# Cross attention in three products of high and low parts, with its last steps in another order

## What is computed

```python
q = (h @ w_xq).reshape(B, S, XATT_HEADS, XATT_HEAD_DIM)        # 4 heads of 256
k, v = jnp.split(mem_n @ w_xkv, 2, axis=-1)                    # same heads
s = jnp.einsum('bshd,bmhd->bhsm', q, k) * (XATT_HEAD_DIM ** -0.5)
p = jax.nn.softmax(s, axis=-1)
o = jnp.einsum('bhsm,bmhd->bshd', p, v)
return o.reshape(B, S, D_MODEL) @ w_xo
```

## Time and profile before

| | us |
|---|---|
| runs | 1096.91, 1097.23, 1099.27; median 1097.23 |
| the profiled execution | 1098.35 |
| its span, first to last instruction | 1096.5 |
| TensorE busy in it | 1085.8 (99%) |
| VectorE, ScalarE, GpSimd busy | 613.4, 562.3, 673.1 |
| granted clock of TensorE | 0.999 of full speed |

### The profile page before, as it was taken

One profiled execution on the slowest core, in us unless ns is written; L12 is line 12 of the kernel. 1 busy time (PEld: TensorE's weight loads), 2 busy tenths in 40 slices (PEclk: granted clock), 3 DMA queues, 4 the chain that ended last, 5 costly groups with the idle time before them and its releaser, 6 DMA issues.

```text
span 1096.5 us, 18883 instructions
## 1 busy us (share of the span) xinstructions
PE 1085.8 (99%) x7591; PEld 984.7 (90%) x7594; DVE 613.4 (56%) x1116; ACT 562.3 (51%) x888; POOL 673.1 (61%) x351
## 2 busy tenths in 40 slices
PE   8999999999999999999999999999999999999997
PEld 7999999998898988888899999999988979888886
DVE  6788579355514642346558877783644345323454
ACT  7545854434645544444464567544346554444443
POOL 4876758627674457754477758685277544686442
PEclk9999999999999999999999999999999999999999
DMA  7544545625653655566555545456266355566563
GB/s 291 174 152 137 177 142 163 174 81 158 195 161 122 211 186 183 190 192 187 178 174 173 157 137 170 145 163 155 77 192 193 96 173 182 186 190 191 183 185 113
DMA packets 63333, 183.31 MB, mean 167 GB/s; under 512 B 18576, under 2 KB 19088, under 8 KB 63248
## 3 DMA queue, kind: packets, MB, share of 16 engines
q1 hardware_dynamic: 47936, 172.48, 49.8%
q10 hardware_dynamic: 15312, 9.64, 3.3%
HBM read 179.47 MB, written 2.62 MB: 166 GB/s over the span
## 4 chain that ended last, share of the span: by engine, by line
PE 96%; DMA 1%; DVE 1%; ACT 1%; POOL 0%; issue 0%; SPq 0%; DVEq 0%; ACTq 0%; POOLq 0%
PE psum L521 22%; PE psum L522 21%; PE psum L523 21%; PE psum L550 12%; PE psum L551 6%; PE psum L695 1%; PE psum L1022 1%; PE psum L1001 1%; PE psum L736 1%; DMA sb_raw<-weights 1%; PE psum L1123 1%; PE psum L625 1%; PE psum L916 1%; PE psum L909 1%; PE psum L791 1%; PE psum L719 1%
## 5 line engine op out<-in xcount | busy, mean ns | idle before, releaser
L418 POOL TENSOR_TENSOR sb_low<-sb_raw,sb_high 128x1024 fp32r<-128x1024 f32 x257 | 619.0, 2423 | 331.4 <-ACT sb_high L408 317.3
L408 ACT ACTIVATE sb_high<-sb_raw 128x1024 fp32r<-128x1024 f32 x322 | 340.2, 1061 | 394.5 <-DMA sb_raw<-weights 355.0
L521 PE MATMUL psum<-sb_h_both,sb_high 128*128 128x256 f32 x1096 | 311.8, 284 | 0.4 <-DVE sb_ff L2304 0.4
L522 PE MATMUL psum<-sb_h_both,sb_high 128*128 128x256 f32 x1096 | 309.9, 283 | 0.0
L523 PE MATMUL psum<-sb_h_both,sb_low 128*128 128x256 f32 x1096 | 309.6, 283 | 0.0
L521 PEld LDWEIGHTS psum<-sb_h_both,sb_high 128*128 128x128 f32 x1096 | 207.4, 189 | 2.0 <-DVE sb_ff L2304 0.8
L523 PEld LDWEIGHTS psum<-sb_h_both,sb_low 128*128 128x128 f32 x1096 | 206.4, 188 | 0.0
L522 PEld LDWEIGHTS psum<-sb_h_both,sb_high 128*128 128x128 f32 x1096 | 206.2, 188 | 0.2
L550 PE MATMUL psum<-sb_h_both,sb_high 128*128 128x512 f32 x544 | 191.8, 394 | 0.0
L551 PE MATMUL psum<-sb_h_both,sb_low 128*128 128x256 f32 x544 | 152.4, 280 | 0.0
L418 DVE TENSOR_TENSOR sb_low<-sb_raw,sb_high 128x1024 fp32r<-128x1024 f32 x65 | 94.6, 1455 | 79.9 <-ACT sb_high L408 79.6
(11 more groups left out here) (314 smaller groups left out, 1699.7 us busy)
## 6 DMA issues: line engine op xcount, KB each, us to landing
sb_raw<-weights SPq DMA_DIRECT2D x322, 512.0 KB, 3.5
sb_pre_gain<-pre_gains ACTq DMA_DIRECT2D x6, 512.0 KB, 5.0
sb_post_gain<-post_gains ACTq DMA_DIRECT2D x6, 512.0 KB, 4.8
sb_kx<-mem SPq DMA_DIRECT2D x2, 512.0 KB, 4.5
sb_x<-x SPq DMA_DIRECT2D x1, 1024.0 KB, 10.7
t_dram<-sb_sq ACTq DMA_DIRECT2D x4, 256.0 KB, 3.0
out<-sb_x SPq DMA_DIRECT2D x4, 256.0 KB, 2.1
m_dram<-sb_m ACTq DMA_DIRECT2D x8, 64.0 KB, 2.1
```

The lines of the kernel that those rows point to most:

```text
L408: nc.scalar.activation(high[:, n % HIGHS, :], raw[:, n % RAWS, :], ACT.Copy).then_inc(high_ready, 1)
L418: eng.tensor_tensor(low[:, k, :], raw[:, k, :], high[:, n % HIGHS, :].bitcast(F32), ALU.subtract).then_inc(low_ready[k], 1)
L521: pe.matmul(out, a[0], b[0], start=start, stop=False, **kw)
L522: pe.matmul(out, a[0], b[1], start=False, stop=False, **kw)
```

## The change

The scores and the outputs go through `product` as well, in three float32r matmuls each, and for this queries, keys, values and turned probabilities are held as high and low parts. ScalarE's copies write the high part; it has two more instructions per layer, the high parts of the keys. VectorE makes all low parts, each in one instruction: four for the values, two for the keys, four for the queries, four for the turned probabilities. TensorE waits for the low parts instead of ScalarE's copies. The new parts lie in places that are free at that time; the low part of the keys and the high part of the values take the place of the numbers themselves. The order of the last steps changes on all three engines: transposes 1 and scores 3 go ahead of output 0, and output 2 is no longer in two pieces around transposes 3, but behind it.

```diff
@@ PE
-                pe.wait_ge(*act_copy.at(layer, ("xq", hd)))
+                pe.wait_ge(*dve_part.at(layer, ("xq_low", hd)))
+                if hd % 2 == 0:
+                    pe.wait_ge(*dve_part.at(layer, ("kx_low", hd // 2)))
                 for c in range(TILES):
                     for b in range(2):
-                        mm = pe.matmul(o[:, c * S:(c + 1) * S], qx[:, 2 * hd + b, c * P:(c + 1) * P], kx[:, 2 * hd + b, :],
-                                       start=(b == 0), stop=(b == 1))
+                        mm = product(o[:, c * S:(c + 1) * S], pick(qx, lambda t: t[:, 2 * hd + b, c * P:(c + 1) * P]),
+                                     pick(kx_parts, lambda t: t[:, 2 * hd + b, :]), b == 0, b == 1)
...
-                o = claim(what, (act_att, what), (6 + hd % 2,))
+                o = claim(what, (dve_part, ("xpt_low", hd)), (6 + hd % 2,))
...
-                    pe.wait_ge(*act_att.at(layer, ("xpt", hd)))
+                    pe.wait_ge(*dve_part.at(layer, ("xpt_low", hd)))
...
                 for b in range(2):
-                    mm = pe.matmul(o[:, part * S:(part + 1) * S], vx[:, b, ...], pxt[:, b, hd, :], ...)
+                    mm = product(o[:, part * S:(part + 1) * S], pick(vx, lambda t: t[:, b, at]), pick(pxt, lambda t: t[:, b, hd, :]), b == 0, b == 1)
...
             cross_scores(2)
+            cross_transposes(1)
+            cross_scores(3)
             cross_out(0, 0)
             cross_out(0, 1)
-            cross_transposes(1)
-            cross_scores(3)
             cross_transposes(2)
             cross_out(1, 0)
             cross_out(1, 1)
+            cross_transposes(3)
             cross_out(2, 0)
-            cross_transposes(3)
             cross_out(2, 1)
@@ ACT
             values_out(1)
+            for half in range(2):
+                nc.scalar.activation(kx_parts[0][:, 4 * half:4 * half + 4, :], kx[:, 4 * half:4 * half + 4, :], ACT.Copy)\
+                    .then_inc(act_copy.sem, act_copy.mark(("kx_high", half)))
...
             cross_exp(2)
+            cross_transposed(1)
+            cross_exp(3)
             cross_out(0)
-            cross_transposed(1)
             cross_transposed(2)
-            cross_exp(3)
             cross_out(1)
@@ DVE
-                for hd in range(3):
-                    x_max(hd)
-                    x_normalise(hd)
+                for half in range(2):
+                    for c in range(TILES):
+                        dve.wait_ge(*act_copy.at(layer, ("xv", c, half)))
+                        to = slice(half * 512, (half + 1) * 512)
+                        V.tensor_tensor(vx[1][:, c, to], bank(("xv", c, half)), vx[0][:, c, to].bitcast(F32), ALU.subtract)\
+                            .then_inc(dve_part.sem, dve_part.mark(("xv_low", c, half)))
+                for half in range(2):
+                    dve.wait_ge(*act_copy.at(layer, ("kx_high", half)))
+                    to = slice(4 * half, 4 * half + 4)
+                    V.tensor_tensor(kx_parts[1][:, to, :], kx[:, to, :], kx_parts[0][:, to, :].bitcast(F32), ALU.subtract)\
+                        .then_inc(dve_part.sem, dve_part.mark(("kx_low", half)))
+
+                def xq_low(hd):
+                    dve.wait_ge(*act_copy.at(layer, ("xq", hd)))
+                    V.scalar_tensor_tensor(out=flat(qx[1][:, 2 * hd:2 * hd + 2, :]), in0=bank(("xq", hd)), scalar=-X_DH ** -0.5,
+                                           in1=flat(qx[0][:, 2 * hd:2 * hd + 2, :]).bitcast(F32), op0=ALU.mult, op1=ALU.subtract)\
+                        .then_inc(dve_part.sem, dve_part.mark(("xq_low", hd)))
+
+                def xpt_low(hd):
+                    dve.wait_ge(*act_att.at(layer, ("xpt", hd)))
+                    V.tensor_tensor(pxt[1][:, :, hd, :], bank(("xpt", hd))..., pxt[0][:, :, hd, :].bitcast(F32), ALU.subtract)\
+                        .then_inc(dve_part.sem, dve_part.mark(("xpt_low", hd)))
+
+                xq_low(0)
+                xq_low(1)
+                x_max(0)
+                x_normalise(0)
+                xq_low(2)
+                x_max(1)
+                x_normalise(1)
+                xpt_low(0)
+                xq_low(3)
+                x_max(2)
+                x_normalise(2)
+                xpt_low(1)
                 x_max(3)
+                x_normalise(3)
                 ox_low(0)
-                x_normalise(3)
-                for hd in range(1, 4):
-                    ox_low(hd)
+                xpt_low(2)
+                ox_low(1)
+                xpt_low(3)
+                ox_low(2)
+                ox_low(3)
```

More of the change, by code:

```diff
@@ L197, in program @@
         ff_t = sb("ff", 2 * 3 * 512, F32R, gates_t)
+        qx_high_t, qx_low_t = sb("qx_high", D * TILES, F32R, gates_t), sb("qx_low", D * TILES, F32R, rb_t)
+        kx_high_t, kx_low_t = sb("kx_high", D * TILES, F32R, y_t), sb("kx_low", D * TILES, F32R, kx_t)
+        vx_high_t, vx_low_t = sb("vx_high", D * TILES, F32R, vx_t), sb("vx_low", D * TILES, F32R, conv_t)
+        pxt_high_t, pxt_low_t = sb("pxt_high", D * TILES, F32R, decay_t), sb("pxt_low", D * TILES, F32R, conv_t, D * TILES)
         psum = ctx.enter_context(nc.psum_tensor("psum", [P, 8, 512], F32))
@@ L210, in program @@
         ff = tuple(ff_t[:, n:n + 3 * 512].rearrange("p (r k t) -> p r k t", r=3, k=2) for n in (0, 3 * 512))
-        vx = vx_t[:, :].rearrange("p (c d) -> p c d", c=TILES)
+        vx = tuple(t[:, :].rearrange("p (c d) -> p c d", c=TILES) for t in (vx_high_t, vx_low_t))
         rope = rope_t[:, :].rearrange("p (w t) -> p w t", w=4)
@@ L267, in program @@
         sel_bias = selb_t[:, :].rearrange("p (c s) -> p c s", c=TILES)
-        qx = gates_t[:, 0:2048].rearrange("p (k t) -> p k t", t=S)
+        qx, kx_parts = (feat(qx_high_t), feat(qx_low_t)), (feat(kx_high_t), feat(kx_low_t))
         px = gates_t[:, 2048:4096].rearrange("p (c h s) -> p c h s", c=TILES, h=X_HEADS)
-        pxt = decay_t[:, :].rearrange("p (b h t) -> p b h t", b=TILES, h=X_HEADS)
+        pxt = tuple(t[:, :].rearrange("p (b h t) -> p b h t", b=TILES, h=X_HEADS) for t in (pxt_high_t, pxt_low_t))
         tiny_at = [0]
@@ L955, in values @@
                     if i % 2 == 0 and 0 in halves:
-                        xv[i // 2] = [claim(("xv", c, i // 2), (act_copy, ("xv", c, i // 2)), (i + c,)) for c in range(TILES)]
+                        xv[i // 2] = [claim(("xv", c, i // 2), (dve_part, ("xv_low", c, i // 2)), (i + c,)) for c in range(TILES)]
                     tall("xv", i, mem_gain, xv[i // 2], halves)
@@ L1018, in cross_out @@
                         ox_banks[hd] = claim(("ox", hd), (dve_part, ("ox_low", hd)), (2 + hd % 2,))
-                        pe.wait_ge(*act_att.at(layer, ("xpt", hd)))
+                        pe.wait_ge(*dve_part.at(layer, ("xpt_low", hd)))
                     o = ox_banks[hd]
+                    at = slice((2 * hd + part) * P, (2 * hd + part + 1) * P)
                     for b in range(2):
-                        mm = pe.matmul(o[:, part * S:(part + 1) * S], vx[:, b, (2 * hd + part) * P:(2 * hd + part + 1) * P], pxt[:, b, hd, :],
-                                       start=(b == 0), stop=(b == 1))
+                        mm = product(o[:, part * S:(part + 1) * S], pick(vx, lambda t: t[:, b, at]), pick(pxt, lambda t: t[:, b, hd, :]), b == 0, b == 1)
                     if part == 1:
@@ L1027, in cross_query @@
                 def cross_query(hd):
-                    wide(("xq", hd), h, (act_copy, ("xq", hd)), (4 + hd % 2,), {} if hd else {4: dve_part.at(layer, ("h_low", "x", 1, 1))})
+                    wide(("xq", hd), h, (dve_part, ("xq_low", hd)), (4 + hd % 2,), {} if hd else {4: dve_part.at(layer, ("h_low", "x", 1, 1))})
                 cross_query(0)
@@ L1312, in values_out @@
                     for c in range(TILES):
-                        copy(vx[:, c, half * 512:(half + 1) * 512], bank(("xv", c, half)), slots, ("xv", 2 * half + 1), act_copy, ("xv", c, half))
+                        copy(vx[0][:, c, half * 512:(half + 1) * 512], bank(("xv", c, half)), slots, ("xv", 2 * half + 1), act_copy, ("xv", c, half))
                 def half_squares(part, product):
@@ L1594, in _ @@
                 values_out(1)
+                for half in range(2):
+                    nc.scalar.activation(kx_parts[0][:, 4 * half:4 * half + 4, :], kx[:, 4 * half:4 * half + 4, :], ACT.Copy)\
+                        .then_inc(act_copy.sem, act_copy.mark(("kx_high", half)))
                 def cross_query(hd):
-                    copy(flat(qx[:, 2 * hd:2 * hd + 2, :]), bank(("xq", hd)), slots, ("xq", hd), act_copy, ("xq", hd), scale=-X_DH ** -0.5)
+                    copy(flat(qx[0][:, 2 * hd:2 * hd + 2, :]), bank(("xq", hd)), slots, ("xq", hd), act_copy, ("xq", hd), scale=-X_DH ** -0.5)
                 def cross_exp(hd):
@@ L1607, in cross_transposed @@
                 def cross_transposed(hd):
```

(7 more changed lines are left out.)

## The result

The changed kernel takes 1099.47 us (median of 20 runs, 1098.54 to 1103.24), the kernel before 1098.16 beside it (20 runs): ratio 1.0016, 95% interval 1.001 to 1.0021, so +1.8 us with 1.1 to 2.3 in the interval (the two medians alone are 1.3 us apart). Forecast were +1.1 us and, against the median known then, 1098.3 in a range of 1094.5 to 1101.2.

What follows compares the result with a forecast made beforehand. TensorE, busy 99% of the span, was taken as the bound. Per layer -2.32 saved, -0.34 old stalls and +3.2 new ones give +0.54, so +1.1 us on 1097.23: 1098.3 us, range 1094.5 to 1101.2.

Steps and rivals of the forecast that it cites:

- The products' saving: Cross attention scores and outputs on TensorE: float32r products save 0.29 us per head's scores or outputs, 2.32 us per layer.
- The work ahead of scores 0: New value, key and query parts before the first scores: hidden, costs nothing; query low 0 near 308.9, scores 0 at 311.1.
- The three stalls behind query 3: TensorE waits for VectorE ahead of scores 3, transposes 3 and output 2: 1.4, 1.0 and 0.8 us per layer.
- the landing ahead of query 3's copy: Load for the fourth xo half, before ScalarE's copy: issued 0.56 us earlier, so its high part starts at 326.75.
- Rival 2: Chain starts later at ScalarE's copy of query 3: landing takes 5.0 us, 1.4 more per layer, 1101.1 us; chance 0.20.
- The sum: Whole cross attention stretch: saving, old stalls gone and new stalls give +0.54 us per layer, +1.1 us in both.
- Rival 1: Behind query 3 the stalls do not come and the products' saving stays: -5.3 us, 1092.0; chance 0.17 in full or good part.
- Rival 3: GpSimd holds off the key lows until 315.27, so scores 0 start 7.3 us later per layer: 1111 us; chance 0.03.

Runs made afterwards that it cites:

- e2: The changed kernel without its 14 low-part instructions per layer, the products taking the high part twice: 1095.28 us, ratio 0.9972 against the kernel before.
- e4: The changed kernel with one more 128x1024 subtraction from SBUF on VectorE behind the key lows: 1101.21 us, ratio 1.0027 against the kernel before.
- e7: The changed kernel with one more 128x512 subtraction from PSUM on VectorE just ahead of query low 3: 1101.92 us, ratio 1.0034 against before.
- e3: The changed kernel with ScalarE's copy of query 3 ahead of the fourth xo half's high part: 1098.18 us, ratio 1.000 against before.
- e6: e5 with minimum 3 and turned lows 2 and 3 moved earlier on VectorE, and new banks for outputs 2 and 3: 1095.15 us, ratio 0.9972.
- e8: The changed kernel with TensorE's and ScalarE's last steps back in the order of before: 1104.55 us, ratio 1.0056 against the kernel before.
- e1: The kernel before with only the change's order of the last steps, plain float32 matmuls, no low parts: 1098.06 us, ratio 0.9997.
- e5: e3 with ScalarE's high part of the fourth xo half deferred behind exponential 3, output 0 and transposed 2: ratio 0.9992 against before.

## Why the prediction was right, point by point

- **The products' saving: right.** 0.29 us per head's scores or outputs were forecast. The measured pitch is even 0.118 instead of 0.12 (scores 2 start at 326.01, the transposes behind them at 327.43: 1.42 us for twelve), and e2 shows the saving in the time.
- **The work ahead of scores 0 costs nothing: right,** to 0.3 us for the end of query low 0 (308.6; 308.9 were forecast, and the whole trace lies some 0.15 later). e4 measured how close the cover's end is.
- **The three stalls behind query 3: right in place and releaser.** Their sizes were 1.4, 1.0 and 0.8 us in the forecast; by the starts they were 1.88, 0.99 and 0.85 in the first layer (output 1 ends at 334.43) and 1.53, 0.98 and 0.85 in the second. e7 and e3 show that they hang on this chain, e6 that the order in it makes them.
- **The term that was mis-sized is the landing ahead of query 3's copy.** The step had it come as much sooner as TensorE did, 0.56 us, at 326.75. The high started at 327.25; the whole trace lies some 0.15 later, so about 0.35 of it is a later landing. In the second layer it is about 0.1, and the stretch is 27.93 for 27.98 forecast. The load itself was issued 0.48 us sooner (323.34; 323.82 before), but the high started 3.91 us behind the issue instead of 3.49. It repeats with the products: in the first layer e2, e7 and e8, with the products, show 3.98, 3.89 and 3.76 us, and e1 with plain matmuls 3.50. Why the landing takes longer is not shown. The chain passed it on in full. Rival 2 named this place; it came with a quarter of the 1.4 us that it put on it, in one layer.
- **The sum.** +0.54 us per layer forecast, +0.85 and +0.50 measured in the stretch, 1.35 together; the runs say 1.8 with 1.1 at the lower end. That the second layer fits so well is partly luck: its three stalls are 3.36 us for 3.2 forecast, and the pitch of 0.118 saves about as much more than forecast (8 x 0.02). Of the 1.2 us between 1098.3 and 1099.47, 0.9 is the median of the kernel before, 1098.16 by twenty runs and 1097.23 by the three known then.
- **The rivals.** Rival 1 (1092.0, by its own terms 1091.9) did not come. e2 and e6, where the chain is gone or cut, go about 3 of its 5.3 us. Rival 3 (keys held off) is refuted by two key lows in 5.01 us; its price should have been two times 7.3 us on top of 1098.3, so 1112.9 and not 1111.
- **One reading.** The 0.15 to 0.2 us from an operand's end to its matmul were read from output 3 in the earlier trace rows, where no start of output 3 is shown. The changed kernel's rows have it: query low 3 ends at 328.82 + 0.69 = 329.51, scores 3 start at 329.66.
- **My error in the experiments:** e3 was expected to win 1.4 to 1.6 us per layer and won 0.76 and 0.62, since I moved the copy without asking what else would then meet: the multiply and GpSimd's low.

## What to carry to other kernels

Where a plain float32 product is replaced by split products, the matmuls get cheaper (0.43 to 0.36 us here), and each operand gets one more instruction between its producer and TensorE; count these in the chain of one head, not as a share of an engine that is 57% busy. Look at what stands ahead of the first link: a copy queued behind a weight's high part cost more here (0.76 and 0.62 us per layer in e3, even with the multiply's new wait) than a subtraction's turn of 0.61, and moving it took one changed number. When a link is moved sooner, check what VectorE and GpSimd then do at the same time; here that took the same limit in three more calls (e5). And when a wait of TensorE has grown, look at the granted clock behind it before the whole loss is put down to the wait.

## What was not expected of the hardware

A float32r matmul of 256 columns took its turn in 0.118 us in scores and outputs (twelve in 1.42), where the earlier trace rows show 0.120 for the weights' products beside it. In e2, whose products take the high part twice, the twelve took 1.44 us again (326.45 to 327.89). What makes the difference is open.

TensorE's granted clock fell twice behind a long wait: to 0.53 from 330.95 to 334.60 in e7, with 2.19 us of idle time ahead of scores 3, and to 0.50 from 711.5 to 714.5 in e5, with 1.97 us. It did not behind the 2.13 us ahead of output 2 in e8's profile, nor behind the 1.63 us in the changed kernel, so the wait's length alone does not decide it. At 0.53 a product of 256 columns took 0.213 us.

VectorE's subtractions with one operand in PSUM ran at 0.69 us next to GpSimd's running lows (query low 0 at 307.93, the value lows at 301.56), while those from SBUF alone waited up to 2.2 us. The Trainium skill (SBUF — State Buffer, section "SBUF: two separate sides") says that a VectorE instruction with two SBUF inputs and a GpSimd instruction that reads SBUF exclude each other for the whole of an instruction. The traces agree (the multiply of e3 ended 0.56 us behind GpSimd's low and took 1.73 us instead of 0.69), and show besides that VectorE gets its turn between two of GpSimd's lows even when these stand back to back (3.43 us for the dose of e4, which are the rest of a low, at most 2.37, and about 1.1 of its own).
